# Scores of a gated linear recurrence in blocks of 32: fewer columns per product, placing moved to ScalarE

## The chip, the cores and the metric

The kernel runs on one core of one Trainium2 chip. The metric is the device time of one execution in microseconds (us). Three executions of the kernel before gave 2228.21 to 2231.21 us, with a median of 2230.57 us.

## What is computed

The reference is two transformer-like blocks over 512 tokens of 1024 channels. The first block (gated delta rule, dilated attention, gated feed-forward) and the Fourier layer of the second are not touched by the change. What matters here is the mixer of the second block, a gated linear recurrence with 16 heads of 128 channels, run forwards and backwards:

```python
def step(S, inp):
    qc, kc, vc, gc = inp
    b = jnp.cumsum(gc, axis=-2)
    diff = b[..., :, None, :] - b[..., None, :, :]
    decay = jnp.exp(jnp.where(causal, diff, -jnp.inf))
    scores = jnp.einsum('bhtc,bhtsc,bhsc->bhts', qc, decay, kc)
    o = (jnp.einsum('bhts,bhsv->bhtv', scores, vc)
         + jnp.einsum('bhtc,bhcv->bhtv', qc * jnp.exp(b), S))
```

Each score of a query t and a key s is a product over 128 channels, where every channel has a decay of its own, the product of the forget gates between s and t. So the scores cannot be one plain matrix product.

## The kernel before

**Levels.** A head's 512 tokens are four chunks of 128 (`TT = 4`, `P = 128`). Inside a chunk the scores are made by halving: at level n (n = 1, 2, 4, ... 64) every pair of neighbouring blocks of n tokens is joined. Keys in one block are scaled by the decay up to the border and queries in the other by the decay from the border, and a product of the scaled keys `KC` and queries `QC` over the channels gives exact scores for that pair of blocks. All other elements of the 128x128 result are meaningless and are masked out. One more product without decay gives the diagonal. That makes eight products a head, li = 0 (diagonal) and li = 1 to 7 (n = 1 to 64).

**TensorE.** `level` (L802) multiplies, per chunk, the 128x128 block of `KC` with that of `QC`, four matmuls in fp32 into one PSUM bank, `bank[4 + li % 2]`. Each fp32 matmul stands in the trace as two weight loads and two matmul records. `scan` (L864) is a generator: after turning the values it gives out the eight levels, then `turn_keys` (L818), `chunk_states` (L828), `inside` (L838) and `output` (L846), one step at a time. The steps of head h-1 are put in between the matmuls of the projection of head h by `unit` (L435): one ahead of each tile after the first, one behind k = 1 and k = 5 of each tile and one ahead of a tile's context part. The projection is three fp32r matmuls of 512 columns per k (L467 to L469) and, for three of the five tiles of a head, three of 256 columns per k for the context (L484 to L486). So the levels of 15 heads lie in the projection of the next head; those of the 16th have nothing around them.

**VectorE.** `start` (L1757) makes the gates `PP`, fills the running decays `QQ` with ones (L1765) and makes the keys `KK`. `produce` (L1770) makes one level's `KC` and `QC` and moves `QQ` and `PP` on to the next; for li = 0 it copies the queries into `QC` (L1782). It waits until the level two before has been multiplied, since `KC` and `QC` have two buffers. `take` (L1813) writes one level's valid elements from the bank into the score tile `MT` with a predicated copy of 128x512 under the mask `hmask[:, li, :]`. In the loop over heads (L1845) it stands inside the production of the level two later, and the last two follow at the end:

```python
for pi in range(2, 8):
    produce(g, pi, (lambda li=pi - 2: take(g, li)))
```

A level may not write its bank before the `take` of two levels before has read it (`lv_bank_free`, L813).

**ScalarE.** It evacuates the projection (L1284 to L1324), makes the high part of each weight tile (L990) and copies the turned keys into `KC` (`place_keys`, L1271). It has no part in `MT`.

Of the kernel before, what the change touches and what calls it, by code (L numbers as in the profile page):

```python
# [41 lines left out]
STEPS = 12  # L42

# [23 lines left out]
def host_constants():  # L67

    i = np.arange(P)
    ident = np.eye(P)  # L70
    upper = (i[:, None] <= i[None, :]) * 1.0
    lev = []
    for h in [1, 2, 4, 8, 16, 32, 64]:
        same = (i[:, None] // (2 * h)) == (i[None, :] // (2 * h))
        first, second = (i // h) % 2 == 0, (i // h) % 2 == 1
        lev.append((same & first[:, None] & second[None, :]) * 1.0)

    cnt = []
# [10 lines left out]
    hm = np.stack(m, 1).astype(np.uint32)  # L89
    c = np.arange(GDIM)  # L90
# [10 lines left out]
    return {"cf": cf, "hm": hm, "dch": dch, "dtok": dtok, "pick": pick}  # L101
# [59 lines left out]
def build(nc, d, out, upto=99, debug=None):  # L161
# [4 lines left out]
    with ctx:  # L166
# [68 lines left out]
        hmask = at("hmask", A0 + 16, [P, 8, P], U32)  # L235
# [97 lines left out]
        def _(sp):  # L333
# [53 lines left out]
            for u in units[NST:]:  # L387
# [6 lines left out]
                if u["lin"] and u["tile"] == T_HG and u["start"]:  # L394

                    sp.wait_ge(S("flo"), FT)
                    sp.dma_start(hmask[:], d["hm"]).then_inc(S("hmask_in"), 16)
# [34 lines left out]
        def _(pe):  # L432
# [113 lines left out]
            for t in range(28):  # L546
# [5 lines left out]
                if t == 22:  # L552
# [6 lines left out]
                    mm.then_inc(S("ba_T"), 1)  # L559
                if t == 23:  # L560

                    pe.wait_ge(S("ba_ev"), 1)
                    for a in range(TT):
                        pe.transpose(bank[3][:, a * 8:a * 8 + 8], rs[0:8, a * P:(a + 1) * P], ident[0:8, 0:8])
                    pe.matmul(bank[3][:, 64:72], ones[0:1, :], t1[0:1, 0:8], start=True, stop=True).then_inc(S("ba_ready"), 1)
                if t == 26:

                    pe.wait_ge(S("g_ready"), 1)
                    pe.matmul(bank[3][:, 80:96], cst[:, 0:P], ggc, start=True, stop=True).then_inc(S("gc_ps"), 1)
# [243 lines left out]
            def lv_bank_free(h, li):  # L813

                if STEPS * h + li >= 2:
                    pe.wait_ge(S("lv_ev%d" % (li % 2)), 6 * h + li // 2)

            def turn_keys(h):  # L818

                pe.wait_ge(S("ke_rdy"), h + 1)  # L820
                for dr in range(2):
                    lv_bank_free(h, 8 + dr)
                    for i in range(3):
                        a = i + dr
                        mm = pe.transpose(bank[4 + dr][:, i * P:(i + 1) * P], QQ[:, dr, a * P:(a + 1) * P], ident[:])
                    mm.then_inc(S("lv_mm"), 1)

            def chunk_states(h):  # L828

                for dr in range(2):  # L830
                    lv_bank_free(h, 10 + dr)
                    for i in range(3):
                        a = i + dr
                        mm = pe.matmul(bank[4 + dr][:, i * P:(i + 1) * P], KC[:, dr, i * P:(i + 1) * P], vt[:, a * P:(a + 1) * P],  # L834
# [3 lines left out]
            def inside(h):  # L838

                pe.wait_ge(S("b6e"), 4 * h + 4)  # L840
                pe.wait_ge(S("lv_ev0"), 6 * h + 4)
                pe.wait_ge(S("lv_ev1"), 6 * h + 4)
# [3 lines left out]
            def output(h):  # L846

                pe.wait_ge(S("qp_rdy"), h + 1)
                pe.wait_ge(S("lv_ev0"), 6 * h + 6)
                pe.wait_ge(S("lv_ev1"), 6 * h + 6)  # L850
# [126 lines left out]
        def _(act):  # L977
# [118 lines left out]
            for t in range(28):  # L1096
# [22 lines left out]
                if t == 23:  # L1119
                    act.wait_ge(S("ba_T"), 1)  # L1120
                    do(A.activation(rs[0:8, :], bank[3][0:8, :], ACT.Copy), "ba_ev")
                if t == 24:

                    act.wait_ge(S("ba_ready"), 1)
# [3 lines left out]
                    do(A.activation(ab[:, 0:4], bank[3][:, 64:68], ACT.Exp), "ba_act")  # L1128
                if t == 25:

                    act.wait_ge(S("sp_abs"), 1)
                    do(A.activation(t2[:, 16:32], t2[:, 16:32], ACT.Exp, scale=-1.0))
                    do.settle()
                    do(A.activation(t2[:, 16:32], t2[:, 16:32], ACT.Ln, bias=1.0), "sp_ln")
                if t == 27:
                    act.wait_ge(S("gc_ps"), 1)
                    do(A.activation(gcc, bank[3][:, 80:96], ACT.Copy))
                    do(A.activation(egc, bank[3][:, 80:96], ACT.Exp), "gcc_ready")
# [132 lines left out]
            def place_keys(g, dr):  # L1271
                act.wait_ge(S("lv_mm"), STEPS * g + 9 + dr)
                do(A.activation(KC[:, dr, 0:3 * P], bank[4 + dr][:, 0:3 * P], ACT.Copy), "lv_ev%d" % dr, 6 * g + 5)
# [10 lines left out]
            for h in range(HG + 1):  # L1284
# [12 lines left out]
                if h < HG:  # L1297
                    for dr in range(2):
# [6 lines left out]
                        if h and dr == 0:  # L1305
                            aux_states(h - 1)
                    finish_tile(t + 3)
# [12 lines left out]
                if h:  # L1320
# [3 lines left out]
                    do(A.activation(vcT[:, 1, :], bank[6][:], ACT.Square), "osq")  # L1324
            head_root(HG - 1)
# [66 lines left out]
        def _(dve):  # L1392
# [114 lines left out]
            for i in range(8):  # L1507
# [6 lines left out]
            dve.wait_ge(S("ba_act"), 1)  # L1514
# [4 lines left out]
            do(X.scalar_tensor_tensor(t2[:, 16:32], t2[:, 0:16], -1.0, t2[:, 0:16], ALU.mult, ALU.max), "sp_abs")  # L1519
            dve.wait_ge(S("sp_ln"), 1)  # L1520
# [4 lines left out]
                                      -1.0, view(ab, [[0, 4], [1, 4]]), ALU.mult, ALU.mult), "g_ready")  # L1525
# [38 lines left out]
            dve.wait_ge(S("gcc_ready"), 1)  # L1564
# [192 lines left out]
            def start(g):  # L1757
# [7 lines left out]
                do(X.memset(QQ[:], 1.0))  # L1765
                do.settle()
                do(X.tensor_scalar(KK[:], PP[:], -1.0, 1.0, ALU.mult, ALU.add))
                do.settle()

            def produce(g, pi, between=None):  # L1770
# [8 lines left out]
                if pi == 0:  # L1779
                    do.settle()  # L1780
                    do(X.tensor_tensor(kc, KK[:, 0, :], KK[:, 1, :], ALU.add))
                    do(X.tensor_copy(qc, q), "lv_rdy")  # L1782
# [30 lines left out]
            def take(g, li):  # L1813

                dve.wait_ge(S("lv_mm"), STEPS * g + li + 1)
                do(X.copy_predicated(MT[:], view(hmask[:, li, :], [[0, 4], [1, P]]),  # L1816
                                     bank[4 + li % 2][:].rearrange("p (a c) -> p a c", c=P)),
                   "lv_ev%d" % (li % 2), 6 * g + li // 2 + 1)

            def states(g):  # L1820

                dve.wait_ge(S("b6e"), 4 * g + 4)
                for i in range(3):
                    for dr in range(2):
# [4 lines left out]
                        else:  # L1829
                            do.settle(1)  # L1830
                        b = bank[4 + dr][:, (a - dr) * P:(a - dr + 1) * P]
                        do(X.scalar_tensor_tensor(ST[:, dr, to, :], ST[:, dr, a, :], PP[:, dr, last:last + 1], b, ALU.mult, ALU.add),
                           "lv_ev%d" % dr if i == 2 else None, 6 * g + 6 if i == 2 else None)
# [11 lines left out]
            for h in range(HG + 1):  # L1845
# [140 lines left out]
```

## Time and profile before

| what | value |
|---|---|
| median of three executions | 2230.57 us |
| profiled execution, its time | 2227.95 us |
| profiled execution, its span | 2226.3 us |
| busy TensorE matmul | 2073.9 us (93%) |
| busy VectorE | 1342.9 us (60%) |
| busy ScalarE | 780.0 us (35%) |
| mean granted TensorE clock | 0.966 |

The span runs from the first to the last instruction; the execution's own time has 1.65 us around it. PE is TensorE, PEld its weight loads, DVE is VectorE, ACT is ScalarE. Busy time is the union of the instructions' durations, and since matmuls overlap in the array, the distance from one start to the next tells what one costs, not its duration. A row of the timeline that stands for several instructions ends with xN; its duration is from the start of the first to the end of the last. A granted clock of 1.00 is 2.4 GHz and 0.50 is 1.2 GHz.

### The profile page before, as it was taken

What the parts mean: (1) busy time and instruction counts of PE and PEld (TensorE: products, weight loads), DVE (VectorE), ACT (ScalarE), POOL (GpSimd) and SP (SyncE); (2) the same over time, 40 slices, a digit from 0 to 9 for tenths busy, and PEclk for the clock granted to TensorE, in tenths of its full rate; (3) what the DMA queues carried; (4) which work ended last, traced back from release to release, by engine and by line L of the source; (5) the groups of instructions that cost most, each with busy time, mean ns of one, the idle gap of its engine ahead of it and who ended that gap; (6) DMA issues with size and microseconds to landing.
All of it is one profiled execution on the core that took longest, in us unless ns stands there. A gap on an engine that the chain in (4) does not pass through costs nothing.

```text
span 2226.3 us, 28314 instructions
## 1 busy us (share of the span) xinstructions
PE 2073.9 (93%) x11523; PEld 1681.5 (76%) x11523; DVE 1342.9 (60%) x2249; ACT 780.0 (35%) x1173; POOL 0.2 (0%) x4
## 2 busy tenths in 40 slices
PE   6998888789999997799999999999999698999997
PEld 4876666567788786688888888888888486787876
DVE  5722676446546565487877888888777733433343
ACT  4354333534324334323333333333333323432233
POOL 0000000000000000000000000000000000000000
PEclk9999899899999999899999999999999799999999
DMA  4331122224534323111111111111111032122321
GB/s 147 95 85 38 59 77 76 86 75 152 157 109 143 93 86 104 38 58 48 48 54 51 48 55 50 48 48 51 55 54 51 10 114 67 48 85 86 85 76 48
DMA packets 286562, 164.63 MB, mean 74 GB/s; under 512 B 6268, under 2 KB 283362, under 8 KB 286434
## 3 DMA queue, kind: packets, MB, share of 16 engines
q1 hardware_dynamic: 286434, 162.83, 24.7%
q8 instruction: 92, 1.51, 0.3%
q14 instruction: 36, 0.29, 0.0%
HBM read 160.71 MB, written 2.10 MB: 73 GB/s over the span
## 4 chain that ended last, share of the span: by engine, by line
PE 72%; DVE 17%; issue 4%; ACT 4%; DMA 1%; SPq 0%; DVEq 0%; ACTq 0%
PE bank L467 17%; PE bank L469 17%; PE bank L468 17%; PE bank L809 3%; DVE KC L1789 2%; DVE MT L1816 2%; DVE QQ L1795 2%; DVE QC L1791 2%; PE bank L486 1%; PE bank L484 1%; PE bank L485 1%; PE bank L925 1%; DMA stage<-in_w_up 1%; PE bank L853 1%; PE bank L834 1%
## 5 line engine op out<-in xcount | busy, mean ns | idle before, releaser
L1409 DVE TENSOR_TENSOR wl<-stage,wh 128x1024 fp32r<-128x1024 f32 (+1 forms) x248 | 301.0, 1215 | 610.2 <-ACT wh L990 610.2
L467 PE MATMUL bank<-hh,wh 128*128 128x512 f32 x1408 | 578.7, 411 | 31.3 <-DVE hl L1430 15.1
L990 ACT ACTIVATE wh<-stage 128x1024 fp32r<-128x1024 f32 (+1 forms) x248 | 260.1, 1051 | 935.3 <-PE bank L469 554.0
L469 PE MATMUL bank<-hh,wl 128*128 128x512 f32 x1408 | 553.7, 393 | 0.0
L468 PE MATMUL bank<-hl,wh 128*128 128x512 f32 x1408 | 552.9, 393 | 0.0
L467 PEld LDWEIGHTS bank<-hh,wh 128*128 128x128 f32 x1408 | 266.9, 190 | 97.1 <-issue 37.3
L469 PEld LDWEIGHTS bank<-hh,wl 128*128 128x128 f32 x1408 | 266.6, 189 | 58.2
L468 PEld LDWEIGHTS bank<-hl,wh 128*128 128x128 f32 x1408 | 267.9, 190 | 48.1 <-issue 0.7
L467 PE MATMUL bank<-gh,wh 128*128 128x512 f32 x432 | 172.3, 399 | 17.2 <-DVE gl L1688 7.3
L469 PE MATMUL bank<-gh,wl 128*128 128x512 f32 x432 | 170.5, 395 | 0.0
L468 PE MATMUL bank<-gl,wh 128*128 128x512 f32 x432 | 170.5, 395 | 0.0
L809 PEld LDWEIGHTS bank<-QC,KC 128*128 128x128 f32 x1024 | 132.0, 197 | 31.1 <-issue 27.5
L809 PE MATMUL bank<-QC,KC 128*128 128x128 f32 x1024 | 141.9, 283 | 14.6 <-DVE MT L1816 12.9
L467 PEld LDWEIGHTS bank<-gh,wh 128*128 128x128 f32 x432 | 82.7, 191 | 37.6 <-DVE gl L1688 8.5
L484 PE MATMUL bank<-ch,wh 128*128 128x256 f32 x384 | 111.1, 289 | 0.0
L485 PE MATMUL bank<-cl,wh 128*128 128x256 f32 x384 | 108.6, 283 | 0.0
L486 PE MATMUL bank<-ch,wl 128*128 128x256 f32 x384 | 108.6, 283 | 0.0
L1789 DVE TENSOR_TENSOR KC<-KK,QQ 128x512 f32<-128x512 f32 x112 | 79.5, 710 | 29.6 <-PE bank L809 29.6
L468 PEld LDWEIGHTS bank<-gl,wh 128*128 128x128 f32 x432 | 82.5, 191 | 17.7 <-issue 0.5
L469 PEld LDWEIGHTS bank<-gh,wl 128*128 128x128 f32 x432 | 82.5, 191 | 17.5
L1816 DVE COPY_PREDICATED MT<-hmask,bank 128x512 f32<-128x512 uint32 x128 | 94.3, 737 | 0.0
L1791 DVE TENSOR_TENSOR QC<-qs,PP 128x512 f32<-128x512 f32 x112 | 79.2, 707 | 0.0
(314 smaller groups left out, 2730.9 us busy)
## 6 DMA issues: line engine op xcount, KB each, us to landing
stage<-in_hg_w_in SPq DMA_DIRECT2D x80, 512.0 KB, 3.6
stage<-in_ada_w SPq DMA_DIRECT2D x48, 512.0 KB, 3.7
stage<-in_w_up SPq DMA_DIRECT2D x44, 512.0 KB, 5.4
stage<-in_ft_w_in SPq DMA_DIRECT2D x32, 512.0 KB, 3.9
stage<-in_w_in SPq DMA_DIRECT2D x28, 512.0 KB, 3.8
stage<-in_w_down SPq DMA_DIRECT2D x16, 512.0 KB, 4.1
stage<-in_hg_w_out SPq DMA_DIRECT2D x16, 512.0 KB, 4.0
stage<-in_ft_w_out SPq DMA_DIRECT2D x16, 512.0 KB, 4.0
```

The source lines that it names most:

```text
L467: pe.matmul(bank[t % NLIN][:], wh[:, s, k, :], xh[:, k, :], start=a, stop=False)
L468: pe.matmul(bank[t % NLIN][:], wh[:, s, k, :], xl[:, k, :], start=False, stop=False)
L469: mm = pe.matmul(bank[t % NLIN][:], wl[:, s, k, :], xh[:, k, :], start=False, stop=b)
L484: pe.matmul(o, wh[:, s, k, :], ch[:, k, :], start=a, stop=False)
L485: pe.matmul(o, wh[:, s, k, :], cl[:, k, :], start=False, stop=False)
L486: mm = pe.matmul(o, wl[:, s, k, :], ch[:, k, :], start=False, stop=b)
L809: mm = pe.matmul(b[:, a * P:(a + 1) * P], kc[:, a * P:(a + 1) * P], qc[:, a * P:(a + 1) * P], start=True, stop=True)
L990: do(A.activation(wh[:, l % NSPLIT, 0:nk, :], stage[:, u["slot"], 0:nk, :], ACT.Copy), "hi_ready")
L1409: do(X.tensor_tensor(wl[:, l % NSPLIT, 0:nk, :], stage[:, u["slot"], 0:nk, :], wh[:, l % NSPLIT, 0:nk, :].bitcast(F32), ALU.subtract), f"s ...
L1789: do(X.tensor_tensor(view(kc[:, 0:1], flat), view(KK[:, 0, 0:1], sel), view(QQ[:, 0, 0:1], sel), ALU.mult))
L1791: do(X.tensor_tensor(view(qc[:, 0:1], flat), view(q[:, 0:1], flat), view(PP[:, 0, 0:1], [[2 * n, nb], [n - T, 2], [1, n]], T), ALU.mult), ...
L1816: do(X.copy_predicated(MT[:], view(hmask[:, li, :], [[0, 4], [1, P]]), bank[4 + li % 2][:].rearrange("p (a c) -> p a c", c=P)), "lv_ev%d" ...
```

## The change

- Levels li = 0 to 5 (the diagonal and n = 1 to 16) only matter inside blocks of 32 tokens on the diagonal. Each is now 16 matmuls of 32 keys by 32 queries, each into its own 32 partitions; a level fills 128 columns of a bank, li = 0 to 3 lie side by side in bank 4 and li = 4, 5 in bank 5.
- li = 6 (n = 32) is 16 matmuls of 32x32 and li = 7 (n = 64) is 8 matmuls of 64x64, all into their places in bank 4, after `take` has read what lay there.
- `take` writes li = 0 to 5 with predicated copies of 128x128 into a compact tile `MC`. They are done two at a time in the production of levels 5, 6 and 7.
- ScalarE gets `place_scores`: one copy of bank 4 (128x512) into `MT`, then four copies of 32 partitions x 128 elements that put `MC`'s blocks on `MT`'s diagonal.
- ScalarE fills `QQ` with ones (`ones_ahead`) in place of VectorE's memset. The copy of the queries for li = 0 is gone; the matmul reads `qs` itself.
- The semaphores are renamed and split to match. `turn_keys` and `chunk_states` use banks 5 and 4 in place of 4 and 5. The mask sent to the core has 6x32 columns in place of 8x128. In the first block only semaphores' names change.

```diff
 def level(h, li):
     pe.wait_ge(S("lv_rdy"), 8 * h + li + 1)
-    lv_bank_free(h, li)
-    b = bank[4 + li % 2]
-    kc, qc = KC[:, li % 2, :], QC[:, li % 2, :]
-    for a in range(TT):
-        mm = pe.matmul(b[:, a * P:(a + 1) * P], kc[:, a * P:(a + 1) * P], qc[:, a * P:(a + 1) * P],
-                       start=True, stop=True)
+    kc, qc = KC[:, li % 2, :], QC[:, li % 2, :] if li else qs[:, h % 2, :]
+    if li < INNER:
+        if h:
+            pe.wait_ge(S("st_ev"), 2 * h if li < 4 else 2 * h - 1)
+        for a in range(TT):
+            for j in range(P // B):
+                tok = slice(a * P + B * j, a * P + B * j + B)
+                to = (li % 4) * P + a * B
+                mm = pe.matmul(bank[4 + li // 4][B * j:B * j + B, to:to + B], kc[:, tok], qc[:, tok], start=True, stop=True)
+    else:
+        w = B if li == INNER else 2 * B
+        pe.wait_ge(S("in_ev"), INNER * h + 4)
+        for a in range(TT):
+            for j in range(P // w):
+                keys, to = a * P + w * j, a * P + w * (j ^ 1)
+                mm = pe.matmul(bank[4][w * j:w * j + w, to:to + w], kc[:, keys:keys + w], qc[:, to:to + w],
+                               start=True, stop=True)
     mm.then_inc(S("lv_mm"), 1)
...
+def place_scores(g):
+    act.wait_ge(S("lv_mm"), STEPS * g + 8)
+    if g:
+        act.wait_ge(S("o_mm"), g)
+    do(A.activation(MT[:], bank[4][:].rearrange("p (a c) -> p a c", c=P), ACT.Copy), "mt_ev")
+    do.settle()
+    act.wait_ge(S("in_ev"), INNER * (g + 1))
+    for j in range(P // B):
+        b = slice(B * j, B * j + B)
+        do(A.activation(MT[b, :, b], MC[b, :, :], ACT.Copy), "mt_ev" if j == P // B - 1 else None)
+
+def ones_ahead(g):
+    do(A.activation(QQ[:], view(ones[:], [[0, 8], [1, P]]), ACT.Copy), "qq_one")
...
 def take(g, li):
-    dve.wait_ge(S("lv_mm"), STEPS * g + li + 1)
-    do(X.copy_predicated(MT[:], view(hmask[:, li, :], [[0, 4], [1, P]]),
-                         bank[4 + li % 2][:].rearrange("p (a c) -> p a c", c=P)),
-       "lv_ev%d" % (li % 2), 6 * g + li // 2 + 1)
+    dve.wait_ge(S("lv_mm"), STEPS * g + (4 if li < 4 else INNER))
+    if g:
+        dve.wait_ge(S("mt_ev"), 2 * g)
+    do.settle()
+    do(X.copy_predicated(MC[:], view(hmask[:, li, :], [[0, TT], [1, B]]),
+                         view(bank[4 + li // 4][:, 0:1], [[B, TT], [1, B]], (li % 4) * P)), "in_ev")
...
-        produce(g, pi, (lambda li=pi - 2: take(g, li)))
+        produce(g, pi, (lambda n=pi: [take(g, li) for li in range(2 * n - 10, 2 * n - 8)]) if pi > 4 else None)
...
-    do.settle(1)
-    take(g, 6)
-    do.settle(1)
+    do.settle()
     do(X.tensor_tensor(KK[:], view(qs[:, g % 2, 0:1], [[0, 2], [1, T]]), PP[:], ALU.mult), "qp_rdy")
-    do.settle(1)
-    take(g, 7)
```

`place_scores(h - 1)` stands in ScalarE's loop between the evacuation of the second forget gate and `finish_tile(t + 3)`; `ones_ahead(h)` is the last thing of each turn of the loop, behind the square of the output (L1324). VectorE's `start` waits for `qq_one` where the memset stood. `turn_keys` waits for all six takes (first direction) and for the copy of bank 4 (second direction); `inside` waits for all of `place_scores`.

## Rows read from the trace of the kernel before

**Rows 1.** The page: busy time by engine, and the chain that ended last, by engine.

```profile
PE 2073.9 (93%) x11523; PEld 1681.5 (76%) x11523; DVE 1342.9 (60%) x2249; ACT 780.0 (35%) x1173; POOL 0.2 (0%) x4
...
PE 72%; DVE 17%; issue 4%; ACT 4%; DMA 1%; SPq 0%; DVEq 0%; ACTq 0%
```

**Rows 2.** Windows: stretch, us; PE, PEld, DVE, ACT, POOL busy; clock; DMA share; GB/s.

```profile
985.00:1732.00 747.00, 734.83 (x4531) 639.98 (x4529) 584.16 (x954) 241.95 (x358) 0.00 (x0) 1.00 0.18 52
...
1732.00:1763.00 31.00, 18.07 (x84) 15.54 (x85) 28.62 (x46) 5.74 (x8) 0.00 (x0) 0.61 0.00 0
```

**Rows 3.** Timeline of PE around one level: start us, us, line, operands, count.

```profile
1327.45 0.28 PE L485 MATMUL bank<-cl,wh 128*128 128x256 f32 x1
1327.57 0.28 PE L486 MATMUL bank<-ch,wl 128*128 128x256 f32 x1
1327.69 1.06 PE L809 MATMUL bank<-QC,KC 128*128 128x128 f32 x8
...
1328.82 0.39 PE L468 MATMUL bank<-hl,wh 128*128 128x512 f32 x1
```

**Rows 4.** Timeline of PE around one set of L450's matmuls with 32 weight columns.

```profile
489.79 0.40 PE L469 MATMUL bank<-hh,wl 128*128 128x512 f32 x1
490.12 1.07 PE L450 MATMUL bank<-stage,silp 128*32 128x256 f32 x16
...
491.46 0.40 PE L468 MATMUL bank<-hl,wh 128*128 128x512 f32 x1
```

**Rows 5.** Timeline of PE, 331.67 to 331.75: the first four records of such a set.

```profile
331.68 0.42 PE L450 MATMUL bank<-stage,silp 128*32 128x256 f32 x4
```

**Rows 6.** Timeline of PE: 32 records in a row with 64 weight columns.

```profile
333.57 0.69 PE L685 MATMUL bank<-g_tt,g_xt 128*64 128x64 f32 x16
334.09 0.64 PE L691 MATMUL bank<-g_xt,g_tt 128*64 128x64 f32 x16
```

**Rows 7.** Timeline of PE: what stands ahead of levels 6 and 7 of a head.

```profile
1341.70 0.40 PE L469 MATMUL bank<-hh,wl 128*128 128x512 f32 x1
1342.31 0.46 PE L809 MATMUL bank<-QC,KC 128*128 128x128 f32 x2 [0.21 <-DVE MT L1816]
...
1345.59 0.39 PE L468 MATMUL bank<-hl,wh 128*128 128x512 f32 x1
1345.81 0.39 PE L469 MATMUL bank<-hh,wl 128*128 128x512 f32 x1
1346.33 1.13 PE L809 MATMUL bank<-QC,KC 128*128 128x128 f32 x8
```

**Rows 8.** Timeline of DVE: the production of level 3 of that head.

```profile
1328.79 0.69 DVE L1789 TENSOR_TENSOR KC<-KK,QQ 128x512 f32<-128x512 f32 x1 [0.64 <-PE bank L809]
```

**Rows 9.** Groups by line and form, DVE, 930 to 1790 us: busy us, mean ns.

```profile
L1832 DVE SCALAR_TENSOR_TENSOR ST<-ST,PP,bank 128x128 f32<-128x128 f32 x96 | 27.6, 343 | 20.7 <-PE bank L834 20.7
```

**Rows 10.** Groups by line and form, ACT: copies of 128x512 and 128x128 from PSUM.

```profile
L1260 ACT ACTIVATE vt<-bank 128x512 f32<-128x512 f32 x16 | 9.5, 592 | 5.6 <-PE bank L781 5.6
...
L1154 ACT ACTIVATE pT<-bank 128x128 f32<-128x128 f32 x8 | 2.2, 275 | 9.9 <-PE bank L599 9.9
```

**Rows 11.** Timeline of ACT: where `place_scores` and `ones_ahead` come to stand.

```profile
1351.82 1.06 ACT L990 ACTIVATE wh<-stage 128x1024 fp32r<-128x1024 f32 x1 [10.09 <-PE bank L486]
...
1368.04 1.06 ACT L990 ACTIVATE wh<-stage 128x1024 fp32r<-128x1024 f32 x1 [4.92 <-PE bank L469]
```

**Rows 12.** Timeline of the last head, which has no projection around it.

```profile
1739.69 2.71 PE L809 MATMUL bank<-QC,KC 128*128 128x128 f32 x16
...
1741.55 0.69 DVE L1789 TENSOR_TENSOR KC<-KK,QQ 128x512 f32<-128x512 f32 x1 [1.98 <-PE bank L809]
...
1744.57 0.68 DVE L1789 TENSOR_TENSOR KC<-KK,QQ 128x512 f32<-128x512 f32 x1
...
1757.81 0.69 DVE L1791 TENSOR_TENSOR QC<-qs,PP 128x512 f32<-128x512 f32 x1
...
1760.88 2.04 PE L809 MATMUL bank<-QC,KC 128*128 128x128 f32 x8 [1.96 <-DVE MT L1816]
```

More of the change, by code:

```diff
@@ L42 @@
 STEPS = 12
+INNER, B = 6, 32
 ROWS = {}
@@ L89, in host_constants @@
     hm = np.stack(m, 1).astype(np.uint32)
+    hc = np.stack([hm[i, :INNER, B * (i // B) + q] for q in range(B)], 2).astype(np.uint32)
     c = np.arange(GDIM)
@@ L234, in build @@
         yB = at("yB", A0, [P, 8, T])
-        hmask = at("hmask", A0 + 16, [P, 8, P], U32)
+        hmask = at("hmask", A0 + 16, [P, INNER, B], U32)
+        MC = at("MC", A0 + 17, [P, TT, B])
         ch = at("ch", A0 + 20, [P, KT, CT], F32R)
@@ L558, in _ @@
                                            stop=(k == KT - 1 and w is w8l))
-                    mm.then_inc(S("ba_T"), 1)
+                    mm.then_inc(S("gate_pe"), 1)
                 if t == 23:
-                    pe.wait_ge(S("ba_ev"), 1)
+                    pe.wait_ge(S("gate_act"), 1)
                     for a in range(TT):
                         pe.transpose(bank[3][:, a * 8:a * 8 + 8], rs[0:8, a * P:(a + 1) * P], ident[0:8, 0:8])
-                    pe.matmul(bank[3][:, 64:72], ones[0:1, :], t1[0:1, 0:8], start=True, stop=True).then_inc(S("ba_ready"), 1)
+                    pe.matmul(bank[3][:, 64:72], ones[0:1, :], t1[0:1, 0:8], start=True, stop=True).then_inc(S("gate_pe"), 1)
                 if t == 26:
-                    pe.wait_ge(S("g_ready"), 1)
-                    pe.matmul(bank[3][:, 80:96], cst[:, 0:P], ggc, start=True, stop=True).then_inc(S("gc_ps"), 1)
+                    pe.wait_ge(S("gate_dve"), 2)
+                    pe.matmul(bank[3][:, 80:96], cst[:, 0:P], ggc, start=True, stop=True).then_inc(S("gate_pe"), 1)
             for a in range(TT):
@@ L830, in chunk_states @@
                 for dr in range(2):
-                    lv_bank_free(h, 10 + dr)
+                    pe.wait_ge(S("ke_ev"), 2 * h + dr + 1)
                     for i in range(3):
                         a = i + dr
-                        mm = pe.matmul(bank[4 + dr][:, i * P:(i + 1) * P], KC[:, dr, i * P:(i + 1) * P], vt[:, a * P:(a + 1) * P],
+                        mm = pe.matmul(bank[5 - dr][:, i * P:(i + 1) * P], KC[:, dr, i * P:(i + 1) * P], vt[:, a * P:(a + 1) * P],
                                        start=True, stop=True)
@@ L1119, in _ @@
                 if t == 23:
-                    act.wait_ge(S("ba_T"), 1)
-                    do(A.activation(rs[0:8, :], bank[3][0:8, :], ACT.Copy), "ba_ev")
+                    act.wait_ge(S("gate_pe"), 1)
+                    do(A.activation(rs[0:8, :], bank[3][0:8, :], ACT.Copy), "gate_act")
                 if t == 24:
-                    act.wait_ge(S("ba_ready"), 1)
+                    act.wait_ge(S("gate_pe"), 2)
                     b3 = bank[3][:, 0:32].rearrange("p (a c) -> p a c", c=8)
@@ L1127, in _ @@
                     do(A.activation(ab[:, 4:8], bank[3][:, 68:72], ACT.Copy))
-                    do(A.activation(ab[:, 0:4], bank[3][:, 64:68], ACT.Exp), "ba_act")
+                    do(A.activation(ab[:, 0:4], bank[3][:, 64:68], ACT.Exp), "gate_act")
                 if t == 25:
-                    act.wait_ge(S("sp_abs"), 1)
+                    act.wait_ge(S("gate_dve"), 1)
                     do(A.activation(t2[:, 16:32], t2[:, 16:32], ACT.Exp, scale=-1.0))
                     do.settle()
-                    do(A.activation(t2[:, 16:32], t2[:, 16:32], ACT.Ln, bias=1.0), "sp_ln")
+                    do(A.activation(t2[:, 16:32], t2[:, 16:32], ACT.Ln, bias=1.0), "gate_act")
                 if t == 27:
-                    act.wait_ge(S("gc_ps"), 1)
+                    act.wait_ge(S("gate_pe"), 3)
                     do(A.activation(gcc, bank[3][:, 80:96], ACT.Copy))
-                    do(A.activation(egc, bank[3][:, 80:96], ACT.Exp), "gcc_ready")
+                    do(A.activation(egc, bank[3][:, 80:96], ACT.Exp), "gate_act")
             for a in range(TT):
@@ L1272, in place_keys @@
                 act.wait_ge(S("lv_mm"), STEPS * g + 9 + dr)
-                do(A.activation(KC[:, dr, 0:3 * P], bank[4 + dr][:, 0:3 * P], ACT.Copy), "lv_ev%d" % dr, 6 * g + 5)
+                do(A.activation(KC[:, dr, 0:3 * P], bank[5 - dr][:, 0:3 * P], ACT.Copy), "ke_ev")
+            def place_scores(g):
[10 more added lines that the diff above has]
+                do(A.activation(QQ[:], view(ones[:], [[0, 8], [1, P]]), ACT.Copy), "qq_one")
             def head_root(g):
@@ L1306, in _ @@
                             aux_states(h - 1)
+                if h:
+                    place_scores(h - 1)
+                if h < HG:
                     finish_tile(t + 3)
@@ L1324, in _ @@
                     do(A.activation(vcT[:, 1, :], bank[6][:], ACT.Square), "osq")
+                if h < HG:
+                    ones_ahead(h)
             head_root(HG - 1)
@@ L1562, in attention_tail @@
                     pair_low(n // 8 - 1)
-            dve.wait_ge(S("gcc_ready"), 1)
+            dve.wait_ge(S("gate_act"), 4)
             up = cst[:, 0:P]
@@ L1764, in start @@
                     dve.wait_ge(S("o_mm"), g)
-                do(X.memset(QQ[:], 1.0))
                 do.settle()
                 do(X.tensor_scalar(KK[:], PP[:], -1.0, 1.0, ALU.mult, ALU.add))
+                dve.wait_ge(S("qq_one"), g + 1)
                 do.settle()
```

35 lines of the change are left out of this document (16 added, 19 removed).

## The prediction

> **What bounds the kernel now.** I read the page first: PE is busy 93% of the span and holds 72% of the chain that ended last, DVE 17% [rows 1]. Then the windows, since the change touches one stage. Over the 747 us in which the levels of 15 heads lie inside projections, PE is busy 98% at the full clock, DVE 78%, ACT 32%; in the last head, alone, DVE is busy 92% and PE 58% at a mean clock of 0.61 [rows 2]. So there are two questions: for 15 heads, what does a level take out of PE's stream; for the last, what does it take out of DVE's. The two are not quite apart. PE stands before levels 6 and 7 of a head: from the last projection matmul to the level's first are 0.61 and 0.52 us, where a 512-column matmul takes 0.228 (1345.59 to 1345.81), so 0.38 and 0.29 us are lost, 0.67 a head, the first named as DVE's predicated copy [rows 7]. DVE's work for level 3 starts the moment level 1 is out of PE [rows 8] and it never idles up to that copy. DVE is therefore a second path almost as long as PE's, and what it saves matters only up to that length.
>
> **PE, price of a level before.** From the last context matmul (1327.57) to the second projection matmul behind the level (1328.82) are 1.25 us; without a level it would be 0.12 (1327.45 to 1327.57) + 0.228. The level takes 0.90 us, which is its 8 records at 0.112 each [rows 3].
>
> **PE, price of an excursion into narrow weights.** L450 is fp32 with 32 weight columns in four column groups, as the new levels are, but with 256 moving columns. From 489.79 to 491.46 are 1.67 us where 0.456 would pass without it: 1.21 us [rows 4]. The four first records start within 0.42 - 0.40 = 0.02 us, 0.007 apart [rows 5], so the groups run at once, and 16 records are four rounds. A round streams 256 columns at 1.2 columns per ns, 0.213 + 0.003 = 0.216; four are 0.864. The rest, 0.344 us, is the price of going in and out (the projection's next weights are not loaded ahead). Both fits hold for other widths: one 128-column record costs 107 + 5 ns [rows 3], a 64-column record 28 (0.64 us for 16 less one's 0.22, over 15), a round of two 56 to 58, which is 53 + 5 [rows 6].
>
> **PE, after.** A 32-column round of four should be 27 + 5 = 32 ns. A level of 16 matmuls is 32 records, 8 rounds, 0.256 us, plus 0.344: 0.60 us against 0.90. The width of the round is not in the trace. Bounds: 0.028 a round, if only issue counts (four times 0.007), and 0.116, if each record costs what a 64-wide one does (four times 0.029). I take 0.032, since L450 has the same weights and groups. Seven levels (0 to 6) save 7 x 0.30 = 2.1 us a head. Level 7 has 16 records of 64 columns, 8 rounds of 0.058 plus about 0.37: 0.83, saving 0.07. Sum 2.17 us.
>
> TensorE's page in the Trainium skill (TensorE: Matmul & The Clock Gate, "Wait — 56ns, not 53.3ns?") says that starts never come closer than about 25 ns however few columns move. By that, were it to hold across column groups, a level would take 32 x 25 + 344 = 1.14 us, an estimate from the page; the four starts within 20 ns [rows 5] disagree, though only in bursts.
>
> **DVE beside PE.** From the start of level 3's keys to the copy that releases level 6 lie four predicated copies of 128x512, about 0.60 each from start to start (a level's five DVE instructions take 3.02 in the last head, [rows 12]). In their place come four of 128x128, each behind a wait for the instruction before it. The nearest row is a 128x128 operation of 0.343 us from PSUM [rows 9]; I take 0.40 with the wait, bounds 0.25 and 0.65. DVE's path shrinks by 4 x 0.20 = 0.8 and starts 0.5 sooner (levels 0 and 1 are over 0.3 and 0.2 us earlier); PE's path up to level 6 shrinks by 5 x 0.30 = 1.5. The stand before level 6 becomes 0.38 + 1.5 - 1.3 = about 0.55 (0 to 1.5 by the bounds). The one before level 7 goes: that level now waits for copies done a level earlier. So 0.67 lost becomes about 0.55, a further 0.12 a head. The memset and the copy of the queries on DVE come before the level 1 wait, and are worth nothing here.
>
> **ACT.** Per head a 128x512 copy (0.592), four small ones (at most 0.275 each) [rows 10] and the ones, 128x1024, about 1.06 like L990: 2.8 us of some 50 us. `place_scores` waits for level 7 (about 1347.5) and then has up to 1351.82, after 10.09 us of idleness; only 1.7 us are needed. What is queued behind it is the third tile's evacuation, which PE ends just before 1351.82. The ones come behind 1362.52 + 0.60 and have up to 1368.04, after 4.92 idle [rows 11]; DVE's `start` is later still. Uncovered, they would cost up to 1.7 and 1.1 us a head. `inside`, which needs `MT`, is three steps behind that. All this I cost at nothing, as also the mask's smaller DMA: SP issues one either way, and nothing waits for it. `turn_keys` and `chunk_states` change banks, not their work. In the first block only names change.
>
> **The last head.** Level 0 holds up DVE until 1741.55; 1.98 us idle [rows 12]. At the low clock 8 records in 1.8 (2.04 less a record's tail) become about 0.8 us in all, so 1.0 less. Then DVE is the path at 3.02 us a level (1741.55 to 1744.57): levels 2, 3 and 4 lose their copy, 3 x 0.6 = 1.8, while 5, 6 and 7 get two small ones for it, no change. Level 7's operands are ready at about 1758.5 and it waits until 1760.88 for a copy [rows 12]; that wait goes, but the keys are now placed behind `place_scores` (0.6 + 4 x 0.275) on ACT: I take 1.5 net. Sum 4.3 us, bounds 0 and 7.
>
> **Sum.** 15 x (2.17 + 0.12) = 34.4, plus 4.3: 39 us. The profiled execution's own time is 2227.95 (span 2226.3), so 2189 by it; the median of three is 2.6 above it. I say 2190.
>
> **Rivals.**
> Short records have a floor like the 64-wide. If a round of four costs 58 ns, a level is 0.344 + 0.464 = 0.81, saving 0.09; seven give 0.63, level 7 0.07. PE's path is then longer than DVE's and all 0.67 of standing goes: 1.35 a head, 20 + 4 = 24 us, 2205. Small copies on DVE at 0.65 end in nearly the same place: the stand grows to 1.5, 2.17 - 0.83 = 1.3 a head, also 2205. For them: the rows know no record with both few weights and few columns. Together 0.17.
>
> The narrow records do not overlap (the other side). Each of the 32 records of a level costs the 0.029 of [rows 6]: 0.344 + 0.928 = 1.27 us, 0.37 more than before. Seven make 2.6, less 0.07 and 0.67: 1.9 a head, 28 us, less 3 in the last head: 25 slower, 2253. It decides from the point where a record costs more than about 0.020 us: 32 x 0.020 + 0.344 = 0.98 is 0.08 over 0.90, times seven the 0.6 that the stands give back. Against it: L450's four starts in 0.02 us. For it: PE then has to be handed 64 instructions in 0.26 us, a rate the rows show only for four in a row. The page TensorEngine Tiling (Array Packing), "Instruction Overhead", in the Trainium skill speaks for this rival: about 60 cycles go with each matmul, and a small dimension should not be tiled. 0.12.
>
> The change does not do what it says: PE's time saved comes back as a stand before another step (`chunk_states`, say, which waits for ACT's keys), and the time stays within a few us, 2228. The idle time on DVE and ACT speaks against it. 0.04.
>
> **How the numbers follow.** The forecast has 0.67, and by its own bounds (round 0.028 to 0.040, small copies 0.25 to 0.50, last head 0 to 7) reaches from 2176 to 2200. With the first rival the range is 2176 to 2212; outside are the other two and the tails, 0.2. A measurement of this kernel tells about 0.2%, 4.5 us, from no change. Faster takes forecast, first rival and a little of the third: 0.85; same 0.03; slower 0.12.
>
> **What the profile after would show.** PE instructions 11523 + 16 x 176 = 14339, DVE 2249 - 64 = 2185, ACT 1173 + 96 = 1269. Right: a 32-wide level's 32 records start within about 0.25 us, the second projection matmul behind a level comes 0.95 us after the last context matmul (1.25 before), a head takes about 2.3 us less, level 6 still waits about half a microsecond for DVE's last small copy, and the last head ends some 4 us sooner. Wrong: 32 records over 0.45 us or more, a level over 0.8 us, or a new stand of PE before `chunk_states` or `inside` on ACT. A granted clock below 1.00 in the 15 heads, where nothing but the levels changed, would also break the sum.

## The result, and the profile after

The changed kernel takes 2192.15 us (median of 4, 2190.57 to 2197.38) against 2230.89 for the kernel before; the ratio is 0.984, with a 95% interval of 0.9825 to 0.9855. Forecast were 2190 us and a range of 2176 to 2212. Run again in a later set of runs, it gave 2192.40 and 0.9844 (0.9829 to 0.9858). The profiled execution took 2193.52 us with a span of 2191.9, so 34.4 us less than the profiled one of before.

The page's busy times and chain, as in [rows 1]:

```profile
PE 2030.0 (93%) x14339; PEld 1613.4 (74%) x14339; DVE 1277.3 (58%) x2185; ACT 824.7 (38%) x1269; POOL 0.2 (0%) x4
...
PE 74%; DVE 15%; issue 5%; ACT 4%; DMA 2%; SPq 0%; DVEq 0%; ACTq 0%
```

The instruction counts are those forecast. PE's share is 93% in both; its busy time fell by 43.9 us with 2816 records more.

To see where the time went I cut both spans at the same three events: the first level of the first head, the first level of the last head, the square of the last head's output (L1324 before, L1357 after). First the windows before:

```profile
959.00:1739.69 780.69, 765.55 (x4724) 667.21 (x4724) 616.55 (x1004) 249.33 (x370) 0.00 (x0) 0.99 0.18 51
1739.69:1769.96 30.27, 19.35 (x107) 17.22 (x106) 23.89 (x41) 3.26 (x6) 0.00 (x0) 0.69 0.00 0
```

and after:

```profile
959.00:1705.64 746.64, 726.00 (x7364) 603.74 (x7362) 553.61 (x941) 291.11 (x461) 0.00 (x0) 1.00 0.19 54
1705.64:1733.37 27.73, 13.18 (x283) 11.52 (x282) 21.09 (x39) 4.86 (x11) 0.00 (x0) 0.61 0.01 1
```

Up to 959 nothing moved. The 15 heads are 34.05 us shorter (forecast 34.4), the last head 2.54 (forecast 4.3), 36.6 together. What lies behind is 2.2 us longer (458.5 against 456.3), though nothing was changed there. The profiled repeat of the changed kernel has 458.8, and the variants of the experiments below lie between 455.6 and 460.8 in no order that follows the change, so the cause of these 2.2 us is not shown. The changed parts thus gave 36.6 us where 39 were forecast; that the medians differ by 38.7 is in part luck.

One 32-wide level in the changed kernel, the answer to [rows 3] and [rows 5]:

```profile
1061.50 0.28 PE L491 MATMUL bank<-ch,wl 128*128 128x256 f32 x1
1061.71 0.46 PE L819 MATMUL bank<-QC,KC 128*32 128x32 f32 x32
1062.10 0.50 PE L472 MATMUL bank<-hh,wh 128*128 128x512 f32 x1
1062.43 0.39 PE L473 MATMUL bank<-hl,wh 128*128 128x512 f32 x1
...
1061.71 0.24 PE L819 MATMUL bank<-QC,KC 128*32 128x32 f32 x4
```

From 1061.50 to 1062.43 are 0.93 us, less 0.348 for two projection starts: 0.58 us (forecast 0.60, before 0.90). The 32 records end 0.22 us after the first four do, so seven rounds of 0.032: the round's cost, the one term that no row of before showed, is what the form 27 + 5 gave. The first four start within 0.02 us again. Each level costs 0.30 to 0.32 us less than it did in the same place before, taken over the 15 heads, and level 7 costs 0.08 less: 2.24 us a head.

Levels 6 and 7, against [rows 7]:

```profile
1074.11 0.40 PE L474 MATMUL bank<-hh,wl 128*128 128x512 f32 x1
1075.22 0.46 PE L827 MATMUL bank<-QC,KC 128*32 128x32 f32 x32 [0.71 <-DVE MC L1854]
...
1078.24 0.39 PE L474 MATMUL bank<-hh,wl 128*128 128x512 f32 x1
1078.56 0.69 PE L827 MATMUL bank<-QC,KC 128*64 128x64 f32 x16
1079.17 0.50 PE L472 MATMUL bank<-hh,wh 128*128 128x512 f32 x1
1079.51 0.39 PE L473 MATMUL bank<-hl,wh 128*128 128x512 f32 x1
```

Level 7 has no wait and costs 1.27 - 0.456 = 0.81 us (forecast 0.83). Level 6 starts 1.11 us behind the last projection matmul where 0.32 is the distance without a wait (1078.24 to 1078.56): a stand of 0.79 us, and the wait is for VectorE's small copy, as forecast, though larger than the 0.55 forecast. VectorE's path to it:

```profile
1062.25 0.69 DVE L1823 TENSOR_TENSOR KC<-KK,QQ 128x512 f32<-128x512 f32 x1 [0.82 <-PE bank L819]
...
1063.46 0.69 DVE L1829 TENSOR_TENSOR QQ<-QQ,PP 128x512 f32<-128x512 f32 x1
1064.18 0.69 DVE L1843 TENSOR_TENSOR PP<-PP 128x512 f32<-128x512 f32 x1
...
1073.52 0.69 DVE L1829 TENSOR_TENSOR QQ<-QQ,PP 128x512 f32<-128x512 f32 x1
1074.34 0.73 DVE L1854 COPY_PREDICATED MC<-hmask,bank 128x128 f32<-128x128 uint32 x2
```

It runs from 1062.25 to 1075.07, 12.8 us, where before it ran from 1328.79 to the release of level 6 at about 1342.2, 13.4. I had it 0.8 us shorter and it is 0.55. A pair of small copies takes 0.73, the 0.37 each being under my 0.40; but in levels 3 and 4 nothing stands between `QQ` and `PP` any more, and the wait for the instruction right before costs 0.12 (1063.46 to 1064.18 is 0.72, not 0.60). Ahead of each pair the gap is larger, 0.22 (1073.52 to 1074.34 is 0.82).

ScalarE's part:

```profile
1079.29 0.60 ACT L1294 ACTIVATE MT<-bank 128x512 f32<-128x512 f32 x1 [4.83 <-PE bank L827]
1079.92 1.31 ACT L1299 ACTIVATE MT<-MC 32x128 f32<-32x128 f32 x4
1083.80 1.06 ACT L1004 ACTIVATE wh<-stage 128x1024 fp32r<-128x1024 f32 x1 [2.57 <-PE bank L491]
...
1094.99 1.06 ACT L1303 ACTIVATE QQ<-ones 128x1024 f32<-128x1024 f32 x1
1100.01 1.06 ACT L1004 ACTIVATE wh<-stage 128x1024 fp32r<-128x1024 f32 x1 [3.96 <-PE bank L474]
```

The placing ends 2.57 us, the ones 3.96 us before the next thing is there to be done; both are hidden in the 15 heads.

### The profile page after: what moved, and what is told of

The parts are those of the page before. It is cut to its first block, busy times and chain, and to the rows that moved or that the text cites. A ratio compares the mean times of both kernels' runs of the same rounds, so it can differ in the third digit from the quotient of the medians.

```text
span 2191.9 us, 34099 instructions
## 1 busy us (share of the span) xinstructions
PE 2030.0 (93%) x14339; PEld 1613.4 (74%) x14339; DVE 1277.3 (58%) x2185; ACT 824.7 (38%) x1269; POOL 0.2 (0%) x4
## 4 chain that ended last, share of the span: by engine, by line
PE 74%; DVE 15%; issue 5%; ACT 4%; DMA 2%; SPq 0%; DVEq 0%; ACTq 0%
PE bank L472 18%; PE bank L474 17%; PE bank L473 17%; DVE KC L1823 2%; DVE QQ L1829 2%; DVE QC L1825 2%; PE bank L489 2%; PE bank L491 1%; PE bank L490 1%; PE bank L939 1%; DMA stage<-in_w_up 1%; PE bank L867 1%; PE bank L850 1%; PE bank L613 1%; ACT wh L1004 1%
## 5 line engine op out<-in xcount | busy, mean ns | idle before, releaser
L1843 DVE TENSOR_TENSOR PP<-PP 128x512 f32<-128x512 f32 x112 | 77.2, 689 | 2.3
L1829 DVE TENSOR_TENSOR QQ<-QQ,PP 128x512 f32<-128x512 f32 x112 | 76.7, 685 | 0.0
L489 PEld LDWEIGHTS bank<-ch,wh 128*128 128x128 f32 x384 | 73.2, 191 | 2.0
```

What stands on the lines that cost most here:

```text
L489: pe.matmul(o, wh[:, s, k, :], ch[:, k, :], start=a, stop=False)
L1829: do(X.tensor_tensor(view(QQ[:, 0, 0:1], [[T + n, 2], [2 * n, nb], [1, n]]), view(QQ[:, 0, 0:1], [[T + n, 2], [2 * n, nb], [1, n]]), view( ...
L1843: do(X.tensor_tensor(view(PP[:, 0, 0:1], [[T - n, 2], [2 * n, nb], [1, n]], n), view(PP[:, 0, 0:1], [[T - n, 2], [2 * n, nb], [1, n]], n), ...
```

## The experiments

The unchanged start of the program, up to the first head, takes 953.8 to 960.4 us in the profiled executions of the kernels below, so a median or a span tells a gain of a few us only roughly. In the traces the most exact measure is the time of one of the 15 heads, from the first value product (L803, before L798) of one head to that of the next. For the changed kernel and the one before:

```profile
1057.29 0.27 PE L803 MATMUL bank<-rs,hf 128*128 128x128 f32 x1
...
1107.23 0.27 PE L803 MATMUL bank<-rs,hf 128*128 128x128 f32 x1
```

```profile
1323.03 0.27 PE L798 MATMUL bank<-rs,hf 128*128 128x128 f32 x1
...
1375.26 0.27 PE L798 MATMUL bank<-rs,hf 128*128 128x128 f32 x1
```

The table gives the median of those distances over 15 heads, from one profiled execution of each kernel. "Last head" is from the last such product to the square of the output.

| kernel | median, us | ratio to before (95%) | a head, us | last head, us |
|---|---|---|---|---|
| before | 2230.89 | | 52.21 | 32.13 |
| changed | 2192.15 | 0.984 (0.9825 to 0.9855) | 49.95 | 29.73 |
| changed, again | 2192.40 | 0.9844 (0.9829 to 0.9858) | 49.92 | 29.70 |
| narrow matmuls only | 2214.13 | 0.9949 (0.9929 to 0.9969) | 51.13 | 32.43 |
| small copies only | 2212.86 | 0.9940 (0.9919 to 0.9961) | 51.36 | 28.96 |
| narrow matmuls twice | 2206.53 | 0.9917 (0.9895 to 0.9938) | 50.97 | 30.30 |
| small copies twice | 2219.72 | 0.9972 (0.9957 to 0.9987) | 51.28 | 31.39 |
| ones on VectorE | 2193.59 | 0.9846 (0.9827 to 0.9866) | 49.92 | 29.81 |
| placing twice | 2190.70 | 0.9836 (0.982 to 0.9853) | 49.93 | 31.06 |
| other bank | 2180.58 | 0.9799 (0.9779 to 0.9818) | 49.14 | 29.30 |
| other bank, keys first | 2174.01 | 0.9752 (0.9734 to 0.9771) | 48.59 | 29.70 |
| and levels 0, 1 together | 2166.10 | 0.9723 (0.9709 to 0.9738) | 48.29 | 29.71 |
| and levels 6, 7 together | 2165.23 | 0.9716 (0.9702 to 0.9731) | 48.07 | 29.19 |

The kernel before was timed afresh on each chip: 2226.22 beside "narrow only", "small copies only", "narrow twice" and "other bank"; 2227.68 beside "again", "ones", "placing" and "keys first"; 2227.27 beside the other three. The repeat was there to compare the later variants on their own chip:

> The changed kernel itself, on the chip of the next three, so that they can be set against it: 1.6 to 1.7% below the kernel before.

**One half of the change at a time.** First the narrow matmuls, with everything else as before:

```diff
-                for a in range(TT):
-                    mm = pe.matmul(b[:, a * P:(a + 1) * P], kc[:, a * P:(a + 1) * P], qc[:, a * P:(a + 1) * P],
-                                   start=True, stop=True)
+                w = 2 * 32 if li == 7 else 32
+                for a in range(TT):
+                    for j in range(P // w):
+                        keys, to = a * P + w * j, a * P + w * (j ^ 1 if li > 5 else j)
+                        mm = pe.matmul(b[w * j:w * j + w, to:to + w], kc[:, keys:keys + w], qc[:, to:to + w],
+                                       start=True, stop=True)
```

> The kernel before with the narrow matmuls alone: li = 0 to 6 as 16 matmuls of 32x32 and li = 7 as 8 of 64x64, each into its own place of the old banks; masks, predicated copies of 128x512 and waits are those of before. Theory (PE's stream and DVE's path to level 6 are two paths of nearly one length): PE saves 2.17 us a head, but DVE's path is not shorter, so the stands before levels 6 and 7 grow from 0.67 to about 2.0 us; net 0.84 a head, 13 us, and about 1 in the last head: some 14 us faster than before. Rival (PE alone sets the pace, the copies on DVE are covered): 2.17 x 15 + 1, some 33 us faster.

Measured: 12.1 us faster than before and 1.08 a head, against 0.84 and 14 us in all expected. PE frees 2.24 us a head and half of it does not arrive; PE spends it standing before levels 6 and 7, 1.22 and 0.67 us where it was 0.37 and 0.29:

```profile
1127.24 0.46 PE L812 MATMUL bank<-QC,KC 128*32 128x32 f32 x32 [1.15 <-DVE MT L1819]
...
1130.26 0.39 PE L469 MATMUL bank<-hh,wl 128*128 128x512 f32 x1
1131.24 0.65 PE L812 MATMUL bank<-QC,KC 128*64 128x64 f32 x15 [0.60 <-DVE MT L1819]
```

The last head was expected to be 1 us shorter and is 0.3 longer; the points further down say why.

Then VectorE's small copies, with the wide matmuls (this kernel leaves out three quarters of the scores):

```diff
-                do(X.copy_predicated(MT[:], view(hmask[:, li, :], [[0, 4], [1, P]]),
-                                     bank[4 + li % 2][:].rearrange("p (a c) -> p a c", c=P)),
+                do(X.copy_predicated(MT[:, :, 0:32], view(hmask[:, li, :], [[0, 4], [1, 32]]),
+                                     view(bank[4 + li % 2][:, 0:1], [[P, 4], [1, 32]])),
```

> The kernel before with each predicated copy cut from 128x512 to 128x128 (three quarters of the scores are not placed; MT is set to zero once); matmuls are those of before. Theory: DVE's path to level 6 is over 1 us shorter, the two stands of 0.67 us a head go and nothing else: 10 us, and 8 x 0.3 = 2.4 in the last head, some 12 us faster than before. Rival (DVE is covered): only the last head's 2.4. Rival (DVE's relief brought most of the 38 us): over 25 faster.

Measured: 13.4 us faster, 0.85 a head and 3.2 in the last (2.4 expected). Level 6 no longer waits:

```profile
1128.26 0.39 PE L469 MATMUL bank<-hh,wl 128*128 128x512 f32 x1
1128.50 0.27 PE L809 MATMUL bank<-QC,KC 128*128 128x128 f32 x1
```

More went than the stands of 0.67. Behind a stand, a 128-wide level's second record starts 0.184 us after the first in place of 0.108 (it is why the first two records of [rows 7] take 0.46), and for two stands that is 0.15 of the difference of 0.18.

So either half alone brings 12 to 13 us, and together 35 to 39: more than the sum, because each uncovers the other. Neither engine alone is "the bound"; the rivals fall, the one with PE alone (33 us), the one in which VectorE is covered (2.4) and the one in which its relief brought most (over 25).

**Each suspected cost doubled.** The matmuls of li = 0 to 5 issued twice:

```diff
-                    for a in range(TT):
+                    for a in [*range(TT), *range(TT)]:
                         for j in range(P // B):
```

> The changed kernel, with the 16 matmuls of each of li = 0 to 5 issued twice (same values). Theory: a round of four costs 0.032 us, so a level costs 0.256 more, 1.54 a head; the stand of 0.79 before level 6 takes up 0.79 of the 1.02 of levels 2 to 5, so 0.75 a head, 11 us, and about 1 in the last head: some 12 us slower than the changed kernel (26 faster than before). Rival (the stand takes nothing up): 23 slower than the changed kernel. Rival (64 instructions more have a cost in being handed to PE): more than 0.256 from first to last record of the second 16.

A head takes 1.02 us more than the changed kernel's (0.75 expected), and the kernel is 19.7 us faster than before (26 expected). The stand is all gone:

```profile
1126.30 0.39 PE L474 MATMUL bank<-hh,wl 128*128 128x512 f32 x1
1126.62 0.27 PE L827 MATMUL bank<-QC,KC 128*32 128x32 f32 x8
```

What differs is the second 16 matmuls:

```profile
1114.33 0.39 PE L474 MATMUL bank<-hh,wl 128*128 128x512 f32 x1
1114.64 0.76 PE L819 MATMUL bank<-QC,KC 128*32 128x32 f32 x64
1115.34 0.50 PE L472 MATMUL bank<-hh,wh 128*128 128x512 f32 x1
...
1114.64 0.46 PE L819 MATMUL bank<-QC,KC 128*32 128x32 f32 x32
```

32 records end after 0.46 us, 64 after 0.76: the second half takes 0.30, not 0.256. Six levels are 1.80 us, and 1.80 less the stand of 0.79 is 1.01, the measured 1.02. The last rival named in the expectation is thus borne out: the first 32 records of a level come 0.008 us apart, four to a round of 0.032, later ones 0.0094 apart on average. That this is the rate at which the instructions are handed to PE fits, but was not tried by itself.

The small copies doubled:

```diff
+                do(X.copy_predicated(MC[:], view(hmask[:, li, :], [[0, TT], [1, B]]),
+                                     view(bank[4 + li // 4][:, 0:1], [[B, TT], [1, B]], (li % 4) * P)))
+                do.settle()
                 do(X.copy_predicated(MC[:], view(hmask[:, li, :], [[0, TT], [1, B]]),
```

> The changed kernel with each of VectorE's six small predicated copies done twice. Theory (DVE's path sets the stand before level 6): four of them lie on that path, each 0.30 us and a wait, about 0.32: 1.3 us a head, 19 us, and 6 x 0.32 less what level 7 covers, 1 to 2, in the last head: some 21 slower than the changed kernel. Rival (DVE has slack of its own): at most 2 slower.

1.33 us a head more (1.3 expected), 1.7 in the last; the span is 2210.3, 18.4 above the changed kernel's (21 expected). The timed executions scatter more than elsewhere (2211.86 to 2225.29), and the profiled one is the fastest of the ten: by the median the kernel is 27.6 us above the changed one, and what the slower executions add is not explained (their mean granted clock goes down to 0.958, from 0.964). In the profiled one VectorE has no slack up to level 6.

**What is hidden.** The ones back on VectorE, and ScalarE's four copies done twice:

```diff
+                do(X.memset(QQ[:], 1.0))
                 do.settle()
                 do(X.tensor_scalar(KK[:], PP[:], -1.0, 1.0, ALU.mult, ALU.add))
-                dve.wait_ge(S("qq_one"), g + 1)
...
-                if h < HG:
-                    ones_ahead(h)
```

> The changed kernel with the ones written by VectorE again (memset of 128x1024, 0.91 us a head) and ScalarE's writing left out. Theory: that memset lies ahead of DVE's wait for level 0, which was 2.2 us long in the profile of the changed kernel, so nothing moves: within 2 us of the changed kernel, in the last head too. Rival (DVE's total work counts): 14 us slower.

```diff
+                for _ in range(1):
+                    for j in range(P // B):
+                        b = slice(B * j, B * j + B)
+                        do(A.activation(MT[b, :, b], MC[b, :, :], ACT.Copy))
+                        do.settle()
                 for j in range(P // B):
```

> The changed kernel with the four small copies of ScalarE done twice (1.3 us and a wait more a head). Theory: ScalarE waits 2.6 us behind them for PE's context part, so the 15 heads hide them; in the last head they lie on the path to the states: 1 to 2 us slower in all. Rival (ScalarE's placing is on the path of every head): 20 slower.

Both as expected: a head takes 49.92 and 49.93 us against 49.92. The memset is taken out of VectorE's own wait; the waits before `KC`, summed, are in the changed kernel and with the ones back:

```profile
DVE KC L1823 <- PE bank L819: 45.3, 31, 2.2
```

```profile
DVE KC L1821 <- PE bank L819: 29.7, 30, 1.3
```

15.6 us less waiting for 16 memsets of 0.912. The last head shows the price of the placing where nothing hides it: 31.06 against 29.70, the 1.3 us of four more copies. In the total this is lost in the scatter (2190.70 and 2192.40, intervals overlapping).

**Taking the stands away.** Levels 0 to 3 go to bank 5, 4 and 5 to bank 3 (which then holds the last head's sum of squares, long read), so that bank 4 is free for level 6:

```diff
-                    if h:
-                        pe.wait_ge(S("st_ev"), 2 * h if li < 4 else 2 * h - 1)
+                    if h and li < 4:
+                        pe.wait_ge(S("st_ev"), 2 * h - 1)
+                    if h and li == 4:
+                        pe.wait_ge(S("ms_ln"), h)
...
-                            mm = pe.matmul(bank[4 + li // 4][B * j:B * j + B, to:to + B], kc[:, tok], qc[:, tok], start=True, stop=True)
+                            mm = pe.matmul(bank[5 - 2 * (li // 4)][B * j:B * j + B, to:to + B], kc[:, tok], qc[:, tok], start=True, stop=True)
...
-                    pe.wait_ge(S("in_ev"), INNER * h + 4)
+                    if h:
+                        pe.wait_ge(S("st_ev"), 2 * h)
```

(and the same bank in `take`)

> The changed kernel with li = 0 to 3 in bank 5, li = 4 and 5 in bank 3 and li = 6 and 7 alone in bank 4, so that level 6 need not wait for the first four small copies. Theory: the stand of 0.79 us before level 6 goes, 12 us faster than the changed kernel (50 faster than before), the last head unchanged within 1. Rival (a later wait, of chunk_states or the next level, takes the stand up): within 3 us of the changed kernel.

```profile
1121.80 0.40 PE L474 MATMUL bank<-hh,wl 128*128 128x512 f32 x1
1122.13 0.46 PE L830 MATMUL bank<-QC,KC 128*32 128x32 f32 x32
```

The stand of 0.79 is gone and a head takes 0.81 us less: the whole of it arrives. The median is 45.6 us below the kernel before (50 expected) and 11.6 below the changed kernel's (12 expected). Next, `place_keys` directly behind `place_scores` on ScalarE:

```diff
                 if h:
                     place_scores(h - 1)
+                    place_keys(h - 1, 0)
+                    place_keys(h - 1, 1)
...
-                if h:
-                    place_keys(h - 1, 0)
-                    place_keys(h - 1, 1)
```

> The kernel with the other bank, and place_keys moved ahead of the third tile's high part and evacuations on ScalarE. Theory: chunk_states then finds its keys, the stand of 0.4 to 0.5 us a head before it goes, 6 to 7 us faster than the kernel with the other bank (some 20 faster than the changed kernel). Rival (the weights' high part, 0.9 us later, is missed by PE): not faster than the kernel with the other bank.

In the changed kernel `chunk_states` (L850) starts 0.70 us after the projection matmul before it, with keys first (L853) 0.23:

```profile
1085.35 0.40 PE L474 MATMUL bank<-hh,wl 128*128 128x512 f32 x1
1086.05 1.16 PE L850 MATMUL bank<-vt,KC 128*128 128x128 f32 x8 [0.30 <-ACT KC L1287]
```

```profile
1132.19 0.39 PE L474 MATMUL bank<-hh,wl 128*128 128x512 f32 x1
1132.42 0.72 PE L853 MATMUL bank<-vt,KC 128*128 128x128 f32 x5
```

0.47 us of stand, and the slower first record behind it (0.213 us to the second in place of 0.108): 0.57, of which 0.55 a head is won. The median is 6.6 us below the one with the other bank (6 to 7 expected), the 15 heads are 8.2 shorter. Last, two excursions joined into one, in `scan`:

```diff
-                for li in range(8):
-                    level(g, li)
-                    yield
+                for lis in ((0, 1), (), (2,), (3,), (4,), (5,), (6,), (7,)):
+                    for li in lis:
+                        level(g, li)
+                    yield
```

> The kernel with other bank and keys first, with level 1 multiplied right behind level 0 in one step (the step after it is left empty). Theory: an excursion into narrow weights costs its 0.33 to 0.34 us of going in and out once less a head: 5 us faster than the kernel it starts from. Rival (the price goes with each level's matmuls, not with the change of width): no difference.

and with `(), (6, 7)` at the end of that list:

> As the one before, and levels 6 and 7 in one step, level 6 moved to level 7's. Theory: a second excursion less, minus what the change from 32 to 64 columns costs, so 0.2 to 0.34 a head: 3 to 5 us faster than with levels 0 and 1 together alone. Rival (level 7 then waits for its operands or ScalarE's placing comes too late): slower than it.

0.30 us a head for the first (0.33 expected), 0.22 for the second (0.2 to 0.34 expected). The price of going in and out goes with the change of width, not with the matmuls; the joined levels give back 0.04 of it, since they have a second 32 records in a row. By the medians the first is 7.9 us faster (5 expected), of which the 15 heads are 4.6. This last kernel is the fastest: 2165.23 us, 0.9716 of before (0.9702 to 0.9731), and 27 us below the changed one. The last step by itself, 0.87 us of the medians, is inside their scatter and stands on the head's time.

## Why the prediction was right, point by point

- **Price of a level.** 0.58 us against 0.60; seven levels save 2.16 and level 7 saves 0.08, 2.24 us where 2.17 was forecast. The price of going in and out, taken from L450's set, held, and joining two levels showed it by itself.
- **The round.** 0.032 us, as the form from three other widths gave. The rival in which a round costs 58 ns falls with the trace; so does the one in which each record costs 29. The decisive row was there before: four starts within 0.02 us [rows 5]. By the Trainium skill, TensorE: Matmul & The Clock Gate, "Wait — 56ns, not 53.3ns?", no two starts come closer than about 25 ns. The trace does not agree for this form: 32 records start within 0.46 - 0.20 = 0.26 us, on average 8 ns apart, so such a floor could hold only within a column group. The Trainium skill's TensorEngine Tiling (Array Packing), "Instruction Overhead", advises against tiling a dimension that is already small. That is not quite this case, as the dimensions were 128 before the cut; but cut down to 32 by 32 a level still gained 0.3 us.
- **The stand before level 6.** The mechanism was right, the size off: "DVE's path shrinks by 4 x 0.20 = 0.8" measured 0.55, since the waits for the instruction right before, in the levels that lost their copy, were left out. The stand became 0.79 in place of 0.55. What makes up for it are the larger gain of the levels (0.07) and the slow first record behind a stand, a term that the sum left out: 0.08 each before levels 6 and 7, and both went, for behind the stand that is left the narrow records come as without one (32 starts in 0.26 us in both). So the closeness of 2.26 us a head to the forecast 2.29 is luck to about 0.2 us.
- **ScalarE, the ones, the queries' copy at nothing.** Right in the 15 heads, by two experiments for ScalarE's placing and the ones. The copy of the queries was not tried alone.
- **The last head.** 4.3 forecast, 2.5 measured. Its first term was right (the wait for level 0). After:

```profile
1705.64 0.66 PE L819 MATMUL bank<-qs,KC 128*32 128x32 f32 x32
...
1706.37 0.69 DVE L1823 TENSOR_TENSOR KC<-KK,QQ 128x512 f32<-128x512 f32 x1 [1.89 <-PE bank L819]
...
1708.91 0.68 DVE L1823 TENSOR_TENSOR KC<-KK,QQ 128x512 f32<-128x512 f32 x1
...
1721.70 0.68 DVE L1825 TENSOR_TENSOR QC<-qs,PP 128x512 f32<-128x512 f32 x1
1722.44 1.12 PE L827 MATMUL bank<-QC,KC 128*64 128x64 f32 x16 [1.04 <-DVE QC L1825]
...
1724.93 1.31 ACT L1299 ACTIVATE MT<-MC 32x128 f32<-32x128 f32 x4 [0.73 <-DVE MC L1854]
...
1726.81 2.93 PE L850 MATMUL bank<-vt,KC 128*128 128x128 f32 x12 [0.31 <-ACT KC L1287]
```

  The keys' products before, and then the stretch of these 12 records before and after (clock in the third place from the end):

```profile
1764.50 1.83 PE L834 MATMUL bank<-vt,KC 128*128 128x128 f32 x12
```

```profile
1764.50:1766.33 1.83, 1.83 (x15) 1.83 (x15) 0.35 (x1) 0.49 (x1) 0.00 (x0) 0.81 0.00 0
```

```profile
1726.81:1729.74 2.93, 2.93 (x13) 2.93 (x14) 0.35 (x1) 0.33 (x1) 0.00 (x0) 0.50 0.00 0
```

  0.73 us in place of 1.86, 1.1 won. Then "3 x 0.6 = 1.8": a level is 2.54 (1706.37 to 1708.91), not 2.42, and the levels with two small copies are over 3.02, so that from this `KC` to level 7's `QC` are 15.33 us against 16.26, 0.9 won. Then "I take 1.5 net" for the end: from that `QC` to the keys' products are 5.11 us against 6.69, 1.58 won, as forecast, though ScalarE waits for VectorE's last copies and places in 1.31. But 1.10 of it is lost again at once, by a term that the sum did not have: the same 12 records of the keys' products take 2.93 us at a granted clock of 0.50, where they took 1.83 at 0.81. In the 5 us ahead of them PE had been busy for 2.64 us, before for 3.38, both at 0.50. The other runs agree: with the wide levels and small copies the 12 take 1.61 us at 1.00, and in all kernels with narrow levels 2.41 to 2.93 at 0.50 to 0.65. So the narrow levels, which leave PE idle longer, are followed by a clock that rises later; that the one causes the other fits every run here and was not tried by itself. It is also why "narrow matmuls only" is not faster in the last head: there these products start 1.05 us sooner and take 2.77. And it is behind the differences of 0.4 to 0.5 us between the last heads of the last four rows of the table.

## What to carry to other kernels

Where two engines' paths to one step are nearly equal, price both: either half of this change alone was worth 12 to 13 us and both 35 or more, and the remaining stand could be read from the trace and taken away whole by giving what the late copies read a bank apart from level 6's. A product of which only blocks on the diagonal are used is cheaper in 32-column pieces spread over the four column groups, even with four times the instructions, as long as the pieces come in long runs: each change of width costs about a third of a microsecond here, more than the run itself (0.25). Where an engine does less, look also at what its clock does behind it: in the last head that took back 1.1 of 3.6 us.

## What the runs showed that was not expected

The first 32 of the narrow records (each with its weight load) come at 32 ns per four, a second 32 right behind them at 37 to 38 ns per four on average (0.30 us). And a stand can cost more than its length: the first of the 128-wide records behind one takes 0.08 to 0.10 us more, the narrow ones no more. Why they differ is not shown.

Part of the price of going in and out can be read from the weight loads. Within the projection a load starts 0.23 us ahead of its matmul, but behind a narrow level the first load starts only 0.12 us after the last narrow record and its matmul together with it.
